# Moving 24 gathered rows of U from the last block to the second one

## The reference, cut to what matters

```python
def block(args):
    xx, ee, gg = args
    hid = jnp.einsum('td,tkd->tk', xx, u[ee].astype(jnp.float32))
    act = jax.nn.gelu(hid, approximate=False) * gg
    return jnp.einsum('tk,tkd->td', act, v[ee].astype(jnp.float32))
```

## Time and profile before

| | |
|---|---|
| Median of 3 runs | 3429.22 us (3426.96 to 3436.71) |
| The profiled execution, its time | 3431.84 us |
| The profiled execution, its span | 3430.0 us |
| Busy share of the span | PE 93%, DVE 63%, POOL 49%, ACT 36% |
| `hidden`, about | from 1016 to 2330 us of the span |
| Block 1 | 1163.8 to 1296.9 us |
| Block 7 | 2149.4 to 2313.0 us |

### The profile page before, as it was taken

How to read it: one execution, slowest core, us unless ns; L and a number is a source line. 1 busy time by engine, 2 the same in 40 slices (tenths; PEclk the granted TensorE clock), 3 DMA queues, 4 the chain that set the end, 5 groups by cost and what they waited for, 6 DMA issues and landing times. The chain is left out here.

```text
span 3430.0 us, 45031 instructions
## 1 busy us (share of the span) xinstructions
PE 3179.5 (93%) x17090; PEld 2875.5 (84%) x17090; DVE 2171.4 (63%) x3550; ACT 1221.7 (36%) x1895; POOL 1690.6 (49%) x847
## 2 busy tenths in 40 slices
PE   7988679998979999999999999994999999999998
PEld 5777668877869999999999999993888888888886
DVE  2510578824445768789897878773666666666664
ACT  3221347722102225656555556561211211112110
POOL 2511010021203565655555555775878778778783
PEclk9999789999999999999999999997999999999999
DMA  3242542041213676677667777888788787787784
GB/s 136 89 167 84 146 105 56 20 169 55 77 35 123 195 239 208 235 249 238 238 233 246 233 246 234 301 312 324 289 305 299 284 297 283 280 312 275 282 305 147
DMA packets 258781, 716.04 MB, mean 209 GB/s; under 512 B 26032, under 2 KB 85296, under 8 KB 251952
## 3 DMA queue, kind: packets, MB, share of 16 engines
q1 hardware_dynamic: 184880, 445.23, 38.1%
q0 software_dynamic: 73728, 268.47, 22.6%
HBM read 578.36 MB, written 135.27 MB: 208 GB/s over the span
## 5 line engine op out<-in xcount | busy, mean ns | idle before, releaser
L956 POOL TENSOR_TENSOR u_lo<-u_raw,u_hi 128x1024 fp32r<-128x1024 f32 x128 | 347.2, 2713 | 442.6 <-ACT u_hi L905 441.7
L1283 PE MATMUL hid_ps<-side_hi,u_hi 128*128 128x384 f32 x2048 | 532.7, 341 | 29.6 <-POOL u_lo L956 18.1
L1214 DVE SCALAR_TENSOR_TENSOR found<-found,x_first 128x1024 f32<-128x1024 f32 x232 | 404.0, 1755 | 230.2 <-DMA found<-in_u,pick_u 229.3
L1283 PE MATMUL hid_ps<-side_lo,u_hi 128*128 128x384 f32 x2048 | 522.9, 336 | 0.2 <-issue 0.2
L1283 PE MATMUL hid_ps<-side_hi,u_lo 128*128 128x384 f32 x2048 | 522.6, 336 | 0.0
L1990 PE MATMUL part<-v_hi,act_hi 128*128 128x512 f32 x1536 | 475.7, 391 | 49.2 <-POOL act_lo L1913 49.2
L1990 PE MATMUL part<-v_lo,act_hi 128*128 128x512 f32 x1536 | 475.0, 390 | 0.0
L1990 PE MATMUL part<-v_hi,act_lo 128*128 128x512 f32 x1536 | 474.3, 390 | 0.0
L1929 DVE TENSOR_TENSOR acc<-acc,part 128x1024 f32<-128x1024 f32 x192 | 234.3, 1220 | 321.2 <-PE part L1990 321.1
L965 POOL DMA_INDIRECT found<-in_u,pick_u x232 | 332.9, 1435 | 209.7 <-DVE found L1214 174.3
L1881 ACT ACTIVATE v_hi<-v_raw 128x2048 fp32r<-128x2048 f32 x64 | 122.8, 1919 | 801.1 <-DMA v_raw<-in_v 617.2
(11 more groups left out here) (213 smaller groups left out, 5187.0 us busy)
## 6 DMA issues: line engine op xcount, KB each, us to landing
u_raw<-in_uT SPq DMA_DIRECT2D x128, 512.0 KB
v_raw<-in_v SPq DMA_DIRECT2D x64, 1024.0 KB
hid_d<-hid SPq DMA_DIRECT2D x128, 384.0 KB
gate_d<-stage SPq DMA_DIRECT2D x48, 1024.0 KB
act_in<-hid_d SPq DMA_DIRECT2D x64, 768.0 KB, 6.5
gate_in<-gate_d SPq DMA_DIRECT2D x32, 1536.0 KB
w_raw<-in_w_in SPq DMA_DIRECT2D x6, 2048.0 KB, 8.3
k_hi<-k_hi_d SPq DMA_DIRECT2D x32, 256.0 KB, 8.0
```

What stands on the lines that cost most here:

```text
L956: pool.tensor_tensor(u_lo[:, s % 2], u_raw[:, :, :], u_hi[:, s % 2].bitcast(F), ALU.subtract).then_inc(u_lo_ok, 1)
L1214: dve.scalar_tensor_tensor(out=found[:, g], in0=found[:, g], scalar=1.0, in1=x_first[:, g], op0=ALU.mult, op1=ALU.mult, accum_out=pick_act ...
L1283: mm = pe.matmul(hid_ps[:, s % 2, half, 0:W], w[:, s % 2, ch], x[:, ch, GB * P + half * W:GB * P + (half + 1) * W], start=n == 0, stop=n = ...
```

## The change

The 24 late picks are gathered and multiplied in block 1 (phase 1) and no longer in block 7. Their two buffers now lie in the first half of `stage`, which nothing uses before block 2. The first late gather of a group waits for the group's picks (`kept`), and ACT waits for all late dots before it first writes `stage` in block 2. The last late dot, one of group 1, stands behind the slots of block 1, ahead of `read_tables`.

```diff
         def late(g):
-            return score[:, g * PEER_HEADS:(g + 1) * PEER_HEADS].rearrange("p h n -> p (h n)")
+            return stage[:, 0, g * SLOTS:(g + 1) * SLOTS].rearrange("p n t -> p (n t)")
...
+                    if phase == GB and s == 0:
+                        for g in range(GB):
+                            act.wait_ge(late_dotted[g], LAG[g])
                     act.wait_ge(gate_mm, j - NO_GATES + 1)
...
                 else:
-                    pool.wait_ge(looked, LOOKS * blocks)
+                    pool.wait_ge(kept, g + 1)
...
-                    if last:
+                    if phase == 1:
                         for g, n in late_picks(s):
                             gather_late(g, n)
...
-                    if last and s:
+                    if phase == 1 and s:
                         for g, n in late_picks(s - 1):
                             dot_late(g, n)
...
-                elif not last:
+                if phase == 1:
+                    for g, n in late_picks(SLOTS - 1):
+                        dot_late(g, n)
+                if phase and not last:
                     read_tables(tb + 1, phase == 1)
...
-            for g, n in late_picks(SLOTS - 1):
-                dot_late(g, n)
```

## The result

| | Before | After |
|---|---|---|
| Median | 3429.62 us (4 runs, 3426.96 to 3436.71) | 3457.38 us (4 runs, 3455.73 to 3458.64) |
| Ratio after / before, 95% | | 1.0074 [1.0059, 1.0089] |
| The profiled execution, its time | 3431.84 us | 3457.14 us |
| Its span | 3430.0 us | 3455.3 us |

The kernel became 0.7% slower. The sum of the prediction was +16.1 us on the profiled execution, the measured difference is 3457.14 - 3431.84 = +25.3 us. The time lies inside the range of 3430 to 3461 us, 12 us above the forecast. There the median was 3453.34 us and the ratio 1.0057 [1.0038, 1.0077].

A forecast was written before the change was run, and what follows sets the result against it. PE, busy nearly throughout blocks 1 and 7, was taken as the bound, with POOL's `u_lo` able to hold it up. Terms 13.2 + 5.5 - 1.3 - 1.3 = +16.1 us on the 3429.22 us median gave 3445 us, range 3430 to 3461.

The forecast's parts named there:

- Part 1: Block 1: with 24 more gathers POOL's period is 9.2 us against PE's slot of 8.32 us, +13.2 us over 15 periods.
- The reason for the gather's price: POOL: a gather seems to write descriptors only between DVE instructions with two SBUF inputs; beside one it takes 2.75 us.
- rival A: Block 1 absorbs the gathers, its period stays within 8.32 us: +2.9 us, 3432 us; chance 0.24, up to small delays.
- Part 2: End of block 1: the last late dot ahead of the tables makes PE take the gates later, +5.5 us.
- Part 3: Block 7: without the late picks PE's one wait there goes, -1.3 us (0 to -1.4).
- Part 4: End of the stage: stores still set the end, one late gather less competes with them, -1.3 us (0 to -1.8).
- B: Block 1 absorbs the gathers and the last late row lands ahead of PE's turn: -2.6 us, 3427 us; chance 0.08.
- C: Block 1 runs like block 7, with a period of 10.35 us: +33.4 us, 3463 us; chance 0.12.
- `u_raw` loop: Past POOL: `u_lo` frees `u_raw`, SP loads, ACT rounds, POOL takes `u_lo`; 9.7 us in block 7, fits 8.32 in block 1.

The follow-up runs named there:

- e1_tables_first: The changed kernel with the last late dot behind block 2's first gate factors and dots, not ahead of the table copies: 3451.46 us, ratio 1.0044 to before.
- e5_one_a_slot: The changed kernel with group 0's 8 late picks in block 0, group 1's 16 one a slot in block 1, last dots behind the tables: 3445.99 us.
- v1_spread: The changed kernel with group 0's 8 late picks in block 0, group 1's split 8 in block 1 and 8 in block 7, even slots: 3439.66 us.
- v2: The changed kernel with 8 late picks in block 0, 4 in block 1, 12 in block 7 (slots 0 to 11): 3431.55 us, ratio 0.9989 to before.

## Why the prediction was right, and where its sizes were off

The direction, the two causes and their places were as predicted. Of the 9.2 us by which the sum was short, 8.0 lie in the first term.

**Part 1, the period of POOL.** In the quiet slots it is what the sum said, 1241.35 - 1232.20 = 9.15 us in the slot shown above. That the two agree so closely is luck, as neither price of a gather was right (below). What failed is to use this period for all 15. In the slots with heavy DVE steps it is 10.0 to 12.1 us, and since POOL's lead over PE is used up early, each of them counts in full. One is at the start: behind the first step of the ranking POOL's wait for the dot grows.

```profile
1173.61 2.40 POOL L959 TENSOR_TENSOR u_lo<-u_raw,u_hi 128x1024 fp32r<-128x1024 f32 x1
1179.59 1.70 POOL L968 DMA_INDIRECT found<-in_u,pick_u  x1 [3.58 <-DVE found L1217]
...
1184.82 2.40 POOL L959 TENSOR_TENSOR u_lo<-u_raw,u_hi 128x1024 fp32r<-128x1024 f32 x1
...
1173.63 4.54 DVE L1068 TENSOR_TENSOR score<-top 128x2048 f32<-128x2048 f32 x1
```

That is a period of 11.2 us (POOL first, then the DVE step behind which the dots stand). Another period, of 10.8 us, comes from a late load of U, for which POOL waits 2.23 us through ACT. The rest are the look-up steps: three periods beside them are 10.0, 11.3 and 12.1 us, the last two with a gather of 3.03 us in each.

By terms of the sum it reads as follows (POOL's groups from 1164 to 1310 us):

```profile
L968 POOL DMA_INDIRECT found<-in_u,pick_u x30 | 49.4, 1645 | 26.2 <-DVE found L1217 21.5 <-issue 4.7
L959 POOL TENSOR_TENSOR u_lo<-u_raw,u_hi 128x1024 fp32r<-128x1024 f32 x15 | 35.8, 2384 | 5.8 <-ACT u_hi L905 5.5 <-issue 0.2
L978 POOL DMA_INDIRECT stage<-in_u,pick_u x22 | 23.4, 1062 | 7.1 <-issue 6.4 <-DVE stage L1224 0.7
```

The ordinary gathers take 1.65 us and not 1.28, the late ones 1.06 and not 1.39. I had taken the ordinary price from a block where few of them met a dot. There DVE mostly had to wait for its second row, and the first gather of a slot found it idle:

```profile
1211.87 1.23 DVE L1214 SCALAR_TENSOR_TENSOR found<-found,x_first 128x1024 f32<-128x1024 f32 x1 [1.09 <-DMA found<-in_u,pick_u]
```

With the change the second dot follows the first at once in nearly every slot, and the first gather beside it takes 1.70 us instead of 0.96. This ordinary dot, and not a late one, is the larger part of the rise. The second gather meets a late dot that makes it dearer only where two of them follow, in every other slot (1.97 us); in the slots with one late dot it takes 0.94 us, as long as no look-up step follows. The late gathers come after the dots and are mostly cheap. With the late gather that the stretch cuts off, all gathers are about 74 us, against 15 x (2 x 1.28 + 1.5 x 1.39) = 69.7 predicted: 4 us. The waits for dots and the steps between gathers are 33.3 us and about 32 were predicted: 1 to 2 us. The waits for ACT's rounding are 5.8 us, of which 2.89 lie ahead of the first period: 2.9 us that the sum had at nothing. Together this is the 8 us and a little more, the little being the rounding of 9.15 to 9.2.

**The reason for the gather's price** held. The Trainium skill, SBUF — State Buffer, Who interferes with whom, infers that descriptor generation isn't held up by a DVE operation on two tensors; by that rule the periods would have been 7.9 us and rival A would have come true. The runs decide against it for these gathers: shorter dots beside it make one fall from 1.97 to 0.94 us, and a shorter look-up step from 3.03 to 1.16 us. In block 1 of after 27 of the 56 gathers take 1.69 us or more, and each of the 27 ends 0.81 to 0.84 us after the end of the two-input DVE instruction in whose time it started. It looks as if they wait for that instruction to end and then need most of their 0.94 us, as the prediction supposed. What exactly is shared was not tried: a gather writes descriptors and also reads its row numbers from `pick_u` in SBUF, and no run tells the two apart.

**Part 2, the late dot ahead of the tables,** was right in mechanism and size. Beyond POOL's delay the gates came 5.5 us late (5.5 predicted), and PE waited 8.83 us there (about 9). That the size fits to 0.1 us is partly luck: the last gather was issued at 1319.21 us, 21.65 us behind the 1297.56 of the prediction and so 1.0 us more than POOL's `u_lo` of slot 32 was late (1311.15 - 1290.50 = 20.65), but its row landed after 5.6 us, at the fast end of the range. Moving that dot alone took 8.4 us from the first gates and 6.7 us for good. What the sum left out is the clock: through the wait PE's granted clock falls to 0.50, its level of 1.2 GHz. The 16 gate products behind it take 3.78 us instead of 1.95, and the products after them start slow. That is +2.6 us, and 2.0 to 2.8 us in each of the other four kernels with a wait of over 8 us. A short wait costs nearly as much: in e1_tables_first, e5_one_a_slot and v1_spread PE waits 2.5 us ahead of the gates of slot 33, the clock falls to 0.50 to 0.58 behind it, and 1.9 to 2.0 us are lost beyond the wait by slot 34.

**Part 3** was right: there is no wait of PE in block 7, POOL's `u_lo` waits for ACT in 15 slots, and the block gives 1.6 us (1.3 predicted) against the first trace of before. Against the second it is 3.1 us; there PE waits twice.

**Part 4** had the right bound and a size that was off. The stores still end the stage: SP waits for them, but for 8.2 instead of the 10.3 us of the earlier trace rows. The gain is 3.2 us (4.5 against the second trace of before), beyond the 1.8 that I gave as the most.

```profile
SPq L893 <- DMA gate_d<-stage: 8.2, 1, 8.2
```

The step that failed is the count of what competes with the stores. I took one late gather. The stretches from the last gelu on, of before and then of after, tell the bytes:

```profile
2311.30:2315.30 4.00, 1.69 (x16) 1.50 (x14) 3.29 (x7) 2.75 (x2) 2.43 (x2) 1.00 0.89 291
2315.30:2319.30 4.00, 0.00 (x0) 0.00 (x0) 1.81 (x3) 0.00 (x0) 0.29 (x1) 0.71 0.97 362
2319.30:2323.30 4.00, 0.00 (x0) 0.00 (x0) 0.41 (x2) 0.00 (x0) 0.00 (x0) 0.50 1.02 426
2323.30:2327.30 4.00, 0.00 (x0) 0.00 (x0) 1.66 (x3) 0.42 (x1) 0.00 (x0) 0.50 1.01 428
2327.30:2330.00 2.70, 0.00 (x0) 0.00 (x0) 0.00 (x0) 0.00 (x0) 0.00 (x0) 0.50 0.29 121
```

```profile
2340.20:2344.20 4.00, 1.67 (x15) 1.48 (x14) 1.38 (x3) 2.91 (x3) 0.00 (x0) 1.00 0.41 162
2344.20:2348.20 4.00, 0.00 (x0) 0.00 (x0) 0.28 (x1) 0.00 (x0) 0.00 (x0) 0.86 0.91 375
2348.20:2352.20 4.00, 0.00 (x0) 0.00 (x0) 0.00 (x0) 0.00 (x0) 0.00 (x0) 0.50 1.01 420
2352.20:2355.70 3.50, 0.00 (x0) 0.00 (x0) 0.00 (x0) 0.00 (x0) 0.00 (x0) 0.50 0.70 290
```

Duration times rate, summed, is 6.36 MB in before and 4.84 MB in after. The difference of 1.51 MB is three gathers of 0.52 MB, and at the 425 GB/s of the full stretches it takes 3.6 us; 3.2 were measured. So it is the backlog of three gathers that was still in flight, not one. They aren't all late ones. In block 7 of before POOL ran behind, so that an ordinary and a late gather were issued after the last gelu (2311.30 us); in after POOL is done 2.9 us ahead of it (2340.18 us). The last gathers, of before and then of after:

```profile
2312.14 1.79 POOL L965 DMA_INDIRECT found<-in_u,pick_u  x1 [1.90 <-DVE found L1214]
2314.66 0.93 POOL L975 DMA_INDIRECT score<-in_u,pick_u  x1 [0.73 <-DVE score L1221]
...
2337.27 0.94 POOL L968 DMA_INDIRECT found<-in_u,pick_u  x1 [2.48 <-DVE found L1217]
```

The account by bytes is rough: the kernel without late picks and v2 move 5.09 and 5.04 MB in this stretch, 0.2 MB more than after, in the same 15.5 us. All kernels with no late pick in the last four slots show 15.5 or 15.6 us here, and v1, with two there, 16.2.

**The rivals.** A and B are out: the periods were not 8.32 us, and PE waited for the tables. C named the right place of the cost and too much of it. The period isn't 10.35 us throughout, but single periods reach it and the mean is 9.73. Its `u_raw` loop showed up once as the bound in after (2.23 us of waiting) and again as soon as the dots were short.

**What stays open.** Blocks 2 to 6 moved by -0.5 to +8.5 us between kernels that are alike there; I haven't found the cause, and it is larger than the gain of the best version. The 3.2 us at the end fit the bytes roughly, but no run changed the bytes there alone, and the kernel before itself differs by 1.3 us there between its two traces.

## What to carry to other kernels

An in-order queue that has a lead over the engine it feeds can take more work only if the sum of its periods fits, the heavy slots with it: add up a whole block with the instructions that will stand side by side, not one quiet slot with the mean prices of a looser block. Don't put a wait for a transfer that was issued a moment ago ahead of what the next phase needs first; behind it, the same dot cost 7 us less. Even a wait of 2.5 us of PE cost some 2 us more by the lower clock behind it. And if small work is to be moved off a full stretch, spread it over the stretches by what room they have, and keep it out of the last slots before a barrier that waits for stores. Here that version was the fastest of those with all picks, but it isn't shown to beat the kernel before.

## What the runs showed of the hardware that I had not expected

- A gather's issue on POOL takes 0.94 us alone. Beside dots of 1.2 us (two inputs from SBUF) it takes 1.70 to 1.97 us, and beside a 2.28 us step of that kind up to 3.03 us. Shortening only the DVE instructions brings it down, to 0.94 and 1.16 us. Beside a reduction of 2.27 us with one input it takes 0.94 us. A long gather ends 0.81 to 0.84 us after the end of the DVE instruction that it met (27 of 27 in block 1 of after).
- A wait of 8.8 us of PE cost 2.6 us more after it had ended, by the lower clock: 16 products in 3.78 us instead of 1.95. A wait of 2.5 us cost 1.9 to 2.0 us more in three kernels. The Trainium skill, TensorE: Matmul & The Clock Gate, What's actually happening, says that the throttled state is the default and activity releases it; the trace agrees, with a granted clock of 0.50 from 1328 us and 1.00 again in the products that follow 1337 us.
- Cutting the late rows to a sixteenth of their bytes, which took the block from 283 to 215 GB/s, changed POOL's delay by 2.5 to 2.9 of 21 us only.
